# A throwaway tanh behind the key norms' square root in a two-layer hybrid decoder trunk

## The chip, the cores and the metric

The kernel runs on one core of a Trainium2 chip. The metric is the time on the device in microseconds, the median of three runs.

## The reference

Two layers on x (256 tokens by 2048, fp32). Each layer has a token mixer and a squared-ReLU MLP, each between two RMS norms. One input projection feeds both halves of the mixer: RWKV-7 (16 heads of 64) and causal attention (8 heads of 128). What matters here is the part that computes a head's keys and decays:

```python
w_log = -jax.nn.softplus(-(w0 + jnp.tanh(wd) @ w2)) - 0.5
decay = jnp.exp(-jnp.exp(w_log.astype(f32)))
a = jax.nn.sigmoid(a0 + ad @ a2)
g = jax.nn.sigmoid(gd) @ g2
...
kk = heads(k * k_k)
kk = kk / jnp.maximum(jnp.sqrt(jnp.sum(kk * kk, axis=-1, keepdims=True)), 1e-12)
k = k * (1 + (a - 1) * k_a)
rh, kh, vh, ah = heads(r), heads(k), heads(v), heads(a)
y = wkv7_scan(rh, heads(decay), kh, vh, -kk, kk * ah)
...
yn = ((y - mu) * lax.rsqrt(var + LNX_EPS)).reshape(bsz, s, c)
```

The key norm and the norm of y need a square root, the decay and the learning rate a sigmoid (written as a tanh) and exps, the attention an exp.

## The kernel before

Every engine's program is written out by hand, one block each, with semaphores between them; each engine works through its own program in order. Weights come by DMA (SyncE's queue) into a ring of four slots, `raw`, of 128x1024 fp32. Per slot, ScalarE makes `whi`, a rounded copy (`hi`, L892), VectorE makes the rest `wlo = raw - whi` (`lo`, L1156), and TensorE (PE) multiplies with both (`tick`, L514, L515 and L517). A slot's `lo` waits for its `hi`, PE waits for both.

The mixer of a layer goes through 8 pairs of RWKV heads, each together with one attention head: the first 7 pairs in a loop, the last written out. While the chain of small operations of pair i runs (`mixer`, a function of this name for each engine), PE fills its time with the input projection of pair i's last group and of pair i+1: 48 ticks over 12 weight slots, a few at each place (`fill`). The calls `step(-1)` to `step(10)` put the 12 `hi` on ScalarE's queue and the 12 `lo` on VectorE's, between the operations of the chain. `finish` empties two PSUM banks of the projection: ScalarE copies one part into `xl` (`halves`, L900), VectorE adds the other (`sums`, L1162), which lets PE write the banks again (`tile_out`).

At the end of pair i, ScalarE does the softmax's exps (L1030), a throwaway one-column square root (L1033), two copies, the square and the root of y's norm (L1039, L1041), and then `key_norms(n + 1)`, the root of the next pair's key norms (L968). Behind it come `step(8)`, `step(9)`, the attention output (L1046), `step(10)` and, once VectorE has gated y, the copy of L1057. The next pair begins with `step(-1)`, `finish(-1)` and the two tanh (L979, L982), three in layer 1 (L985), then three exps (L987 to L989).

VectorE's order at the same place: the norm of y (to L1425), `step(8)`, the gating (L1438, L1440), the attention's low part (L1429), the low part of y (L1446), `step(9)`, `step(10)`; in the next pair `finish(-1)` (L1162), the clamp (L1265) and the reciprocal (L1267) of the key norms, then L1270, the first user of the tanh, the scan (L1272), and the chain that ends at L1309 with what PE transposes at L649. In each layer `key_norms` is called once before the loop as well, for the first pair. PE's order: the ticks of the last group, the small lora matmuls (L628 to L630, in layer 1 L632 too), then seven ticks that wait for `tile_out`, then L639 and L649.

The key-norm root and the tanh of the next pair use different tables of ScalarE; the instruction that loads one (ACT_TABLE_LOAD) is put in by the compiler, in front of the activation that needs it, and bears its line. `spare` is a 128x1 tile that nothing reads; `col_eps` is a constant column.

Of the kernel before, what the change touches and what calls it, by code (L numbers as in the profile page):

```python
# [32 lines left out]
ACT = mybir.ActivationFunctionType  # L33
# [74 lines left out]
def trunk(nc, consts, levels, x, norm_mix_pre, norm_mix_post, norm_mlp_pre, norm_mlp_post, w_in, w_in_vres,  # L108
          shift_mu, shift_mu_vres, decay_w0, decay_w2, iclr_a0, iclr_a2, vres_v0, vres_v2,
          gate_g2, k_k, k_a, r_k, lnx_gain, lnx_bias, w_out, w_up, w_down, out):  # L110
    with ExitStack() as ctx:
        def sb(name, shape, dt=F32):
            return ctx.enter_context(nc.sbuf_tensor("b_" + name, shape, dt))
# [51 lines left out]
        spare = sb("spare", [P, 1])  # L165
# [21 lines left out]
        col_eps, col_lnx = cst[:, C_COL + 2:C_COL + 3], cst[:, C_COL + 3:C_COL + 4]  # L187
# [693 lines left out]
        def _(act):  # L881
            f = nc.scalar.activation
# [82 lines left out]
            def key_norms(n):  # L965

                act.wait_ge(e["n2_sum"], n + 1)
                f(rn[:, :], mb[0][:, SEQ:2 * SEQ], ACT.Sqrt).then_inc(e["n2_root"], 1)  # L968

            def mixer(l, i, n, tiles, step, finish, more=True):  # L970

# [70 lines left out]
                if more:  # L1042
                    key_norms(n + 1)
# [19 lines left out]
            for l in range(DEPTH):  # L1063
# [17 lines left out]
                def turn(i):  # L1081
                    def finish(g):

                        halves(k + 11 + 4 * g, i * 3, t + 4 + 2 * g + i * 6, (2, 2, 0)[g + 1])
                    mixer(l, i, PAIRS * l + i, t + 4 + i * 6, lambda j: hi(k + 8 + j + LEAD, i * 3), finish)
                key_norms(PAIRS * l)
                loop(act, PAIRS - 1, turn)

# [543 lines left out]
```

## Time and profile before

| | |
|---|---|
| median of three runs | 2646.45 us |
| lowest, highest | 2644.17, 2647.09 us |
| the profiled execution's own time | 2645.33 us |
| its span, first to last instruction | 2643.7 us |
| its mean granted clock of TensorE | 0.994 |
| busy share: PE, VectorE, ScalarE, GpSimd | 98%, 64%, 46%, 4% |
| weights and other data moved by DMA | 419.96 MB, mean 159 GB/s |

All rows below are of one profiled execution. PE's busy time overlaps itself, since matmuls are pipelined and their ends are modelled; so the waits of PE are read rather than its busy time. A timeline's row gives the start and the duration, both in microseconds; instructions of one line that follow each other are merged ("x2"). On ScalarE and VectorE an instruction may start a little before the one ahead of it ends.

### The profile page before, as it was taken

What the parts mean: (1) busy time and instruction counts of PE and PEld (TensorE: products, weight loads), DVE (VectorE), ACT (ScalarE), POOL (GpSimd) and SP (SyncE); (2) the same over time, 40 slices, a digit from 0 to 9 for tenths busy, and PEclk for the clock granted to TensorE, in tenths of its full rate; (3) what the DMA queues carried; (4) which work ended last, traced back from release to release, by engine and by line L of the source; (5) the groups of instructions that cost most, each with busy time, mean ns of one, the idle gap of its engine ahead of it and who ended that gap; (6) DMA issues with size and microseconds to landing.
All of it is one profiled execution on the core that took longest, in us unless ns stands there. A gap on an engine that the chain in (4) does not pass through costs nothing.

```text
span 2643.7 us, 48415 instructions
## 1 busy us (share of the span) xinstructions
PE 2585.5 (98%) x16267; PEld 2118.7 (80%) x16267; DVE 1680.0 (64%) x2761; ACT 1210.2 (46%) x1896; POOL 116.4 (4%) x183
## 2 busy tenths in 40 slices
PE   7999999999999999999899999999999999999998
PEld 6777777778888888888687777777788888888886
DVE  5767666657656556566567766676576565564665
ACT  5444445445434444344454444454454344443443
POOL 3000000000000000000010000100000000000000
PEclk9999999999999999999999999999999999999999
DMA  6443333365555555555544333333655655555554
GB/s 199 117 117 110 108 105 97 122 216 174 189 192 184 192 188 183 200 183 191 171 117 119 106 113 105 97 98 120 215 175 190 192 183 192 190 181 199 185 189 150
DMA packets 437898, 419.96 MB, mean 159 GB/s; under 512 B 19503, under 2 KB 351937, under 8 KB 437825
## 3 DMA queue, kind: packets, MB, share of 16 engines
q1 hardware_dynamic: 434176, 412.49, 49.1%
q0 software_dynamic: 3648, 6.52, 0.9%
q8 instruction: 44, 0.72, 0.1%
q14 instruction: 30, 0.24, 0.0%
HBM read 416.84 MB, written 2.10 MB: 158 GB/s over the span
## 4 chain that ended last, share of the span: by engine, by line
PE 91%; DVE 6%; ACT 1%; issue 1%; DMA 0%; DVEq 0%; SPq 0%; ACTq 0%
PE gemm_bank L514 29%; PE gemm_bank L515 15%; PE gemm_bank L539 11%; PE gemm_bank L541 11%; PE gemm_bank L540 11%; PE gemm_bank L517 2%; PE mix_banks L661 1%; PE mix_banks L687 1%; DVE b_rn L1267 1%; DVE b_wlo L1156 1%; PE mix_banks L694 1%; PE mix_banks L733 1%; PE mix_banks L737 1%; PE mix_banks L744 1%; PE mix_banks L740 1%
## 5 line engine op out<-in xcount | busy, mean ns | idle before, releaser
L1156 DVE TENSOR_TENSOR b_wlo<-b_raw,b_whi 128x1024 fp32r<-128x1024 f32 x777 | 940.2, 1223 | 561.0 <-ACT b_whi L892 558.8
L514 PE MATMUL gemm_bank<-b_hT,b_whi 128*128 128x512 f32 x3420 | 1253.5, 407 | 2.2 <-DVE b_zt L1162 2.2
L892 ACT ACTIVATE b_whi<-b_raw 128x1024 fp32r<-128x1024 f32 x777 | 810.1, 1057 | 609.2 <-PE gemm_bank L541 428.4
L515 PE MATMUL gemm_bank<-b_hT,b_wlo 128*128 128x256 f32 x3648 | 1012.7, 281 | 0.0
L514 PEld LDWEIGHTS gemm_bank<-b_hT,b_whi 128*128 128x128 f32 x3420 | 643.2, 188 | 171.3 <-issue 22.4
L515 PEld LDWEIGHTS gemm_bank<-b_hT,b_wlo 128*128 128x128 f32 x3648 | 689.5, 189 | 10.7
L539 PE MATMUL gemm_bank<-b_whi,b_mT 128*128 128x512 f32 x1280 | 501.6, 392 | 0.0
L541 PE MATMUL gemm_bank<-b_whi,b_mT 128*128 128x512 f32 x1280 | 498.3, 389 | 0.0
L540 PE MATMUL gemm_bank<-b_wlo,b_mT 128*128 128x512 f32 x1280 | 498.2, 389 | 0.0
L539 PEld LDWEIGHTS gemm_bank<-b_whi,b_mT 128*128 128x128 f32 x1280 | 240.3, 188 | 51.3 <-issue 1.4
L541 PEld LDWEIGHTS gemm_bank<-b_whi,b_mT 128*128 128x128 f32 x1280 | 240.3, 188 | 50.3
L540 PEld LDWEIGHTS gemm_bank<-b_wlo,b_mT 128*128 128x128 f32 x1280 | 240.3, 188 | 48.7
L900 ACT ACTIVATE b_xl<-gemm_bank 128x256 f32<-128x256 f32 x229 | 75.1, 381 | 149.1 <-PE gemm_bank L517 145.1
L1021 ACT ACTIVATE b_U<-mix_banks 64x128 f32<-64x128 f32 x64 | 17.4, 271 | 223.9 <-PE mix_banks L733 223.9
L1115 ACT ACTIVATE b_mT<-b_AR 128x256 f32 (+1 forms) x128 | 48.3, 418 | 111.8 <-DVE b_AR L1561 111.8
L1002 ACT ACTIVATE b_yo<-mix_banks 128x256 f32<-128x256 f32 x80 | 30.7, 384 | 143.1 <-PE mix_banks L694 143.1
L1555 DVE TENSOR_TENSOR b_AR<-gemm_bank,b_xl 128x256 f32<-128x256 f32 x128 | 48.5, 420 | 62.2 <-ACT b_xl L900 62.1
L517 PE MATMUL gemm_bank<-b_hT,b_whi 128*128 128x512 f32 x228 | 85.1, 395 | 0.0
L1565 DVE TENSOR_TENSOR b_mT<-b_AR,b_mT 128x256 f32 (+1 forms) x128 | 50.9, 424 | 26.4 <-ACT b_mT L1115 25.9
L1162 DVE TENSOR_TENSOR b_zt<-gemm_bank,b_xl 128x256 f32<-128x256 f32 x101 | 38.2, 420 | 37.8 <-ACT b_xl L900 37.0
L687 PEld LDWEIGHTS mix_banks<-b_yo 64*64 64x64 f32 x1280 | 44.6, 134 | 21.1 <-issue 21.1
L694 PE MATMUL mix_banks<-b_yo 64*64 64x64 f32 x1536 | 60.8, 225 | 0.0
(238 smaller groups left out, 1895.8 us busy)
## 6 DMA issues: line engine op xcount, KB each, us to landing
b_raw<-in_w_up SPq DMA_DIRECT2D x256, 512.0 KB
b_raw<-in_w_down SPq DMA_DIRECT2D x256, 512.0 KB
b_raw<-in_w_in SPq DMA_DIRECT2D x384, 256.0 KB
b_raw<-in_w_out SPq DMA_DIRECT2D x60, 512.0 KB
b_raw<-in_w_in SPq DMA_DIRECT2D x8, 512.0 KB
b_xt<-in_x SPq DMA_DIRECT2D x4, 512.0 KB, 6.0
b_raw<-in_w_out SPq DMA_DIRECT2D x8, 256.0 KB
out<-b_xt SPq DMA_DIRECT2D x8, 256.0 KB, 2.3
```

What stands on the lines that cost most here:

```text
L514: mm(bank[b0 + b][:, :], whi[r][:, cols], pair, start=first, stop=False)
L515: m = mm(bank[b0 + b][:, 0:SEQ], wlo[r][:, cols], act[:, kt, 0, :], start=False, stop=False)
L517: m = mm(bank[b0 + b][:, :], whi[r][:, cols], pair, start=False, stop=True)
L539: mm(bank[b0 + u][:, :], mT[:, kt, 0, toks], whi[r][:, cols], start=first, stop=False)
L540: mm(bank[b0 + u][:, :], mT[:, kt, 0, toks], wlo[r][:, cols], start=False, stop=False)
L541: m = mm(bank[b0 + u][:, :], mT[:, kt, 1, toks], whi[r][:, cols], start=False, stop=last)
L687: mm(mb[2 + h][to, CHUNK * u:CHUNK * u + CHUNK], old, Z[rows, lv, 2 * h + u, :], start=True, stop=True)
L694: m = mm(mb[h][to, CHUNK * u:CHUNK * u + CHUNK], Z[rows, lv, 2 * h + u, :], old, start=True, stop=True)
L892: f(whi[r][:, :], raw[r][:, :, :].rearrange("p a b -> p (a b)"), ACT.Copy).then_inc(hi_done, 1)
L900: f(xl[:, b, :], bank[b0 + b][:, SEQ:2 * SEQ], ACT.Copy).then_inc(half_out, 1)
L1156: tt(wlo[r][:, :], flat(raw[r][:, :, :]), whi[r][:, :].bitcast(F32), ALU.subtract).then_inc(lo_done, 1)
L1565: tt(mT[:, at, 1, :], hid(b).unsqueeze(1), mT[:, at, 0, :].bitcast(F32), ALU.subtract).then_inc(tile_out, 1)
```

## The change

One line is added to `key_norms` on ScalarE: a tanh of one constant column into `spare`, behind the root. It signals nobody. It runs wherever `key_norms` is called: once before the loop of each layer, and in each of the 7 loop turns, so 16 times.

```diff
                 act.wait_ge(e["n2_sum"], n + 1)
                 f(rn[:, :], mb[0][:, SEQ:2 * SEQ], ACT.Sqrt).then_inc(e["n2_root"], 1)
+                f(spare[:, :], col_eps, ACT.Tanh)
 
             def mixer(l, i, n, tiles, step, finish, more=True):
```

## Rows read from the trace of the kernel before

**Rows 1.** The page: busy time of each engine; chain that ended last, by engine.
```profile
PE 2585.5 (98%) x16267; PEld 2118.7 (80%) x16267; DVE 1680.0 (64%) x2761; ACT 1210.2 (46%) x1896; POOL 116.4 (4%) x183
...
PE 91%; DVE 6%; ACT 1%; issue 1%; DMA 0%; DVEq 0%; SPq 0%; ACTq 0%
```

**Rows 2.** Groups of instructions by line (columns as in the page), ScalarE.
```profile
L979 ACT ACT_TABLE_LOAD x16 | 20.5, 1283 | 0.3
```

**Rows 3.** Timeline, ScalarE, one seam: start, duration (us), instruction, [idle before <- releaser].
```profile
282.00 0.19 ACT L1030 ACTIVATION_READ_ACCUMULATOR b_sm<-b_sm,b_small 128x1 f32 x1
282.21 1.28 ACT L1033 ACT_TABLE_LOAD   x1
...
283.71 0.38 ACT L1035 ACTIVATE b_AKV<-mix_banks 128x256 f32<-128x256 f32 x1
...
285.48 0.36 ACT L968 ACTIVATE b_rn<-mix_banks 128x256 f32<-128x256 f32 x1
285.74 2.00 ACT L892 ACTIVATE b_whi<-b_raw 128x1024 fp32r<-128x1024 f32 x2
...
287.90 1.06 ACT L892 ACTIVATE b_whi<-b_raw 128x1024 fp32r<-128x1024 f32 x1
288.97 0.42 ACT L1057 ACTIVATE b_mT<-b_yf 128x256 f32 x1
...
291.98 0.66 ACT L900 ACTIVATE b_xl<-gemm_bank 128x256 f32<-128x256 f32 x2 [1.53 <-PE gemm_bank L517]
292.66 1.28 ACT L979 ACT_TABLE_LOAD   x1
293.95 0.47 ACT L979 ACTIVATE b_eN<-mix_banks,b_drv 128x256 f32<-128x256 f32 x1
```

**Rows 4.** Timeline, VectorE, the same seam.
```profile
286.82 1.23 DVE L1156 TENSOR_TENSOR b_wlo<-b_raw,b_whi 128x1024 fp32r<-128x1024 f32 x1 [0.58 <-ACT b_whi L892]
...
289.64 0.42 DVE L1446 TENSOR_TENSOR b_mT<-b_yf,b_mT 128x256 f32 x1 [0.47 <-ACT b_mT L1057]
289.98 2.35 DVE L1156 TENSOR_TENSOR b_wlo<-b_raw,b_whi 128x1024 fp32r<-128x1024 f32 x2
292.40 0.76 DVE L1162 TENSOR_TENSOR b_zt<-gemm_bank,b_xl 128x256 f32<-128x256 f32 x2
...
293.39 1.75 DVE L1267 RECIPROCAL b_rn<-b_rn 128x256 f32<-128x256 f32 x1
295.06 0.23 DVE L1270 TENSOR_SCALAR b_ldc<-b_eN 128x256 f32<-128x256 f32 x1
```

**Rows 5.** Timeline, TensorE matmuls, the same seam.
```profile
288.87 0.40 PE L514 MATMUL gemm_bank<-b_hT,b_whi 128*128 128x512 f32 x1
...
293.41 0.47 PE L514 MATMUL gemm_bank<-b_hT,b_whi 128*128 128x512 f32 x1 [0.29 <-DVE b_zt L1162]
```

**Rows 6.** Timelines, VectorE and TensorE, start of layer 0's first pair.
```profile
59.59 0.76 DVE L1162 TENSOR_TENSOR b_zt<-gemm_bank,b_xl 128x256 f32<-128x256 f32 x2 [4.05 <-ACT b_xl L900]
...
60.60 0.47 PE L514 MATMUL gemm_bank<-b_hT,b_whi 128*128 128x512 f32 x1 [0.48 <-DVE b_zt L1162]
```

**Rows 7.** Timeline, VectorE, a seam of layer 1.
```profile
1428.96 2.35 DVE L1156 TENSOR_TENSOR b_wlo<-b_raw,b_whi 128x1024 fp32r<-128x1024 f32 x2
1431.44 0.76 DVE L1162 TENSOR_TENSOR b_zt<-gemm_bank,b_xl 128x256 f32<-128x256 f32 x2
```

**Rows 8.** Waits of TensorE: who was waited for, total us, times, longest.
```profile
PE mix_banks L649 <- DVE b_btl L1309: 7.1, 8, 1.0
```

**Rows 9.** TensorE's timeline; stretches (length, busy us by engine, clock, DMA share, GB/s).
```profile
593.33 1.09 PE L563 MATMUL mix_banks<-b_cst,b_xt 128*128 128x128 f32 x8 [3.10 <-DVE b_xt L1176]
...
595.00:595.50 0.50, 0.50 (x5) 0.50 (x4) 0.50 (x2) 0.50 (x2) 0.00 (x0) 0.50 0.00 0
601.50:602.00 0.50, 0.50 (x5) 0.46 (x4) 0.50 (x3) 0.50 (x1) 0.50 (x1) 0.87 0.17 33
234.00:292.00 58.00, 57.53 (x499) 44.70 (x497) 40.69 (x89) 26.74 (x53) 3.85 (x7) 1.00 0.38 111
```

## The prediction

> **What bounds the kernel now.** I read the page first: TensorE (PE) is busy for 98% of the span, VectorE (DVE) for 64%, ScalarE (ACT) for 46%, and the chain that ended last is PE for 91% and DVE for 6% [rows 1]. So time spent or saved on ScalarE is worth something only at a place where PE waits, at the end of some chain, for ScalarE. Next, the groups of instructions on ScalarE: a table load takes 1283 ns each time, and 16 of them stand before the tanh at L979, one for each pair of heads, 8 pairs in each of 2 layers [rows 2]. In the seam a second one stands before the throwaway square root at L1033, and the copies behind either have none [rows 3], so copies run on either table. Then the timelines of the three engines around one seam between two pairs, the one at 283 to 296 us, which is where the change acts [rows 3 to 5]. The reader should look there for instructions that start within some hundredths of a microsecond of the end of what they wait for: those have no slack, and whatever delays the one delays the other.
>
> The chain at the seam. ScalarE does the key norms' square root (L968) and then at once the conversion `hi` of weight slot 8 (L892, at 285.74, ends near 286.80) [rows 3]. VectorE has been idle for 0.58 us for it and starts the matching `lo` (L1156) at 286.82 [rows 4]. VectorE's queue is in order: behind that `lo` stand the gating of the pair's output, the split of L1446, two more `lo`, then the two sums that empty the PSUM banks (L1162, 292.40), the clamp and the reciprocal of the key norms (L1267), and only then the line that needs the tanh (L1270) [rows 4]. PE, at 293.41, has been idle for 0.29 us for L1162 [rows 5], because its next group of weights overwrites those banks. So hi(8), lo(8), the tail of VectorE, L1162 and PE form one chain.
>
> **The change part by part.** *What is added:* behind each of the 16 key-norm roots, a table load and a one-column tanh. The nearest row is the same pair of instructions with a square root, at L1033: the load starts at 282.21, 0.02 us after its predecessor ends (282.00 + 0.19), and the instruction behind the throwaway one starts at 283.71, so 1.52 us go by from the end of the one to the start of the next [rows 3]. Without the pair, the next instruction begins 0.10 us before its predecessor ends (L968 ends at 285.48 + 0.36 = 285.84, L892 starts at 285.74) [rows 3]. So hi(8) comes 1.52 + 0.10 = 1.62 us later; the lower bound is 1.50, load and tanh alone, with none of the overlap lost.
>
> *What is removed:* the load of L979, since its table is now in place when the next pair begins. There are as many loads as before: 16 are moved, none is dropped. What it is worth must be read where the tanh is used. In the seam the tanh ends at 293.95 + 0.47 = 294.42, but L1270 starts at 295.06, just when the reciprocal releases VectorE (293.39 + 1.75 = 295.14, with the usual 0.08 of overlap) [rows 3, 4]. The tanh is 0.64 us early already; coming 1.28 us earlier still, it is worth nothing. The a-tanh and the exps come behind, and wait for VectorE too.
>
> *Is 1.62 us absorbed on the way?* ScalarE has 1.53 us idle before its L900 [rows 3], and that hides its own lateness there almost wholly, but it is the wrong place: the loss is passed on to VectorE 6 us before that, through lo(8). On VectorE the 0.58 us before lo(8) is the wait itself. The idle time before L1446 (0.47) is a wait for ScalarE's L1057, which stands behind hi(10) (287.90 + 1.06 = 288.96, start 288.97) [rows 3, 4]; hi(10) is 1.62 later as well. Two `lo` then run to 289.98 + 2.35 = 292.33, could give way at 292.25 with the overlap of 0.08, and L1162 starts at 292.40 because the first half of L900 ends near 292.36 [rows 3, 4]: slack 0.15. In layer 1 the same working gives 1428.96 + 2.35 − 0.08 = 1431.23 against 1431.44, slack 0.21 [rows 7]. I take these two for all loop seams of their layers.
>
> *What else is late.* PE needs lo(8) for the last 16 matmuls of its group, which start near 288.9 [rows 5]. lo(8) now ends at 286.82 + 1.23 = 288.05, and would end at 289.67, so PE stops there for 0.8 us, and L900 moves from 291.98 to about 292.8. Its first half is ready near 293.2, before VectorE is free at 292.25 + 1.62 = 293.87, so this stall doesn't add; it is part of the same 1.62. The load of the next weights into the slot is issued after lo(8), so 1.6 us later, and is used after L1270, which is as late. The normalised output that PE transposes (L785) needs no ScalarE work behind the new tanh. So nothing else grows.
>
> *Layer 0, 7 loop seams:* PE waits for L1162 already [rows 5], thus 1.62 − 0.15 = 1.47 us each. *Layer 1, 7 loop seams:* PE has a fourth small matmul and doesn't wait at L1162, but it waits some 0.9 us (7.1 / 8) for VectorE at L649, 8 times in this trace, the longest 1.0 us [rows 8], so there VectorE's lateness arrives whole: 1.62 − 0.21 = 1.41 us each. *The first pair of each layer, 2 times:* hi and L900 follow L968 on ScalarE, VectorE sits idle for 4.05 us until L900 and PE 0.48 us until VectorE [rows 6]: no slack, 1.62 us each. The sum: 7 × 1.47 + 7 × 1.41 + 2 × 1.62 = 10.3 + 9.9 + 3.2 = 23.4 us.
>
> Nothing is given back later: between seams PE is busy for 57.53 of 58 us [rows 9], so there is no idle time that a late start could use up. The profiled execution took 2645.33 us (span 2643.7), 1.1 less than the median of 2646.45; the sum on the profiled one is 2668.7, on the median 2669.9. I predict 2669.9.
>
> *A rule against the row.* The rows show a load of 1.28 us with neighbours 0.01 to 0.02 us away on both sides [rows 3]. The Trainium skill, ScalarE: Activation LUTs, section What ACT_TABLE_LOAD costs, puts a drain of some 1380 ns beside each load, 2.66 us for a switch; an estimate from that page would make each seam 1.38 us worse and the whole change some 22 us worse again, near 2692 us in all. The trace doesn't show such a drain, so I don't add it.
>
> **The rivals.**
> *Faster, with the tanh as the last to arrive:* the change would gain if, at L1270, VectorE waited for the tanh, and if the load at its new place fell in idle time. Then the 1.28 us of each load goes: 16 × 1.28 = 20.5 us, 2626 us. For it: ScalarE's 1.53 us idle before L900. Against it: the 0.64 us by which the tanh is early, and lo(8) 0.02 us behind hi(8). It decides where hi(8) is needed 1.6 us later than it is done. Chance 0.03.
>
> *Hidden:* the delay of lo(8) is swallowed by VectorE before L1162, which it can do only if the 0.47 and 0.58 us of idle are no consequence of ScalarE. No gain, no loss: 2646 us. Chance 0.07. Partly hidden (one idle time of the two, about 0.5 us in each loop seam): 14 × 0.5 = 7 us less, 2663; chance 0.05.
>
> *The table load stays at L979 too* (the change doesn't do what it says, because the table isn't known at the loop's head): then ScalarE has 1.28 us more, but the tanh would end near 293.4 + 1.28 + 0.47 = 295.1, against 296.6 when the late VectorE wants it. The time is the forecast's, the loads are up to 16 more. If instead the throwaway tanh were dropped, the time would be 2646; the one at L1033 is kept, so this is in "hidden".
>
> *Costlier, by the clock:* PE's granted clock fell from 1.00 to 0.50 (2.4 to 1.2 GHz) after a stop of 3.10 us that ended at 593.33: it was 0.50 at 595.0 and nearly back in the slice from 601.5 [rows 9]. At most 6.5 us of matmuls ran at half of the clock, which costs up to 3.3 us; I take 2.5, since part of it was idle. If a stop of about 1.9 us, in two pieces, did this at every seam, it would add 16 × 2.5 = 40 us: 2710. Against it: each piece is at most a good third of that stop (0.8 and 1.1 against 3.10), and a whole pair, with its stops at both ends, runs at a granted clock of 1.00 now [rows 9]. Chance 0.05.
>
> **How the numbers follow.** Forecast 0.80, partly hidden 0.05, costlier 0.05, hidden 0.07, faster 0.03. The forecast's own bounds: with 1.50 inserted instead of 1.62 the sum is 1.9 less; with no slack at all 2.5 more; and the runs of the kernel before lie up to 2.3 from their median: 2666 to 2675. With the partly hidden case the range is 2661 to 2676. Faster by over 0.2% (what a measurement of this kernel can tell from no change) 0.03, within it 0.07, slower 0.90.
>
> **What would show it.** Right: 16 loads at the new line, none at L979; VectorE's idle time before lo(8) at each loop seam 0.58 + 1.62 = 2.2 us instead of 0.58; PE idle before its first L514 some 1 us instead of 0.29 and a new stop of 0.8 us near the end of the group before it; L1270 straight behind the reciprocal; each pair 1.4 to 1.5 us longer. Wrong: if VectorE's L1162 starts less than 1 us later against the pair's own root, something on VectorE had slack that I took for a wait on ScalarE; if L1270 comes to wait for the tanh, the tanh's place in the chain was misread; if the clock's row shows less than 1.00 between pairs, the last rival.

## The result, and the profile after

The changed kernel takes 2668.47 us (median of four runs, 2666.64 to 2669.13), against 2646.44 for the kernel before: 22.0 us more, a ratio of 1.0084 with a 95% interval of 1.0066 to 1.0101. It is slower, by about what was forecast (2669.9). The profiled execution took 2666.64 us, its span is 2665.0, so between the two profiled executions there are 21.3 us. The times of the experiments below are medians too; the kernel before, run anew beside them, took 2646.43 us beside e1 to e4 and 2646.88 beside e5 to e8, and their ratios are to these.

The first look is ScalarE's timeline at the seam that answers to [rows 3] (a row is start, duration, instruction, idle time before). Lines from L969 on have moved down by one, so L979 of before is L980 here, and VectorE's L1156, L1162, L1267 and L1270 are L1157, L1163, L1268 and L1271.

```profile
292.81 0.36 ACT L968 ACTIVATE b_rn<-mix_banks 128x256 f32<-128x256 f32 x1
293.19 1.28 ACT L969 ACT_TABLE_LOAD   x1
294.49 0.20 ACT L969 ACTIVATE b_spare<-b_cst 128x1 f32<-128x1 f32 x1
294.60 1.99 ACT L892 ACTIVATE b_whi<-b_raw 128x1024 fp32r<-128x1024 f32 x2
...
300.19 0.66 ACT L900 ACTIVATE b_xl<-gemm_bank 128x256 f32<-128x256 f32 x2 [0.88 <-PE gemm_bank L517]
300.82 0.47 ACT L980 ACTIVATE b_eN<-mix_banks,b_drv 128x256 f32<-128x256 f32 x1
```

The load now stands behind the root, and none stands between L900 and L980. hi(8) starts 1.79 us after the root starts (294.60 − 292.81); it was 0.26 [rows 3]. The same places on VectorE, which answer to [rows 4]:

```profile
295.67 1.23 DVE L1157 TENSOR_TENSOR b_wlo<-b_raw,b_whi 128x1024 fp32r<-128x1024 f32 x1 [2.09 <-ACT b_whi L892]
...
298.49 0.43 DVE L1447 TENSOR_TENSOR b_mT<-b_yf,b_mT 128x256 f32 x1 [0.46 <-ACT b_mT L1058]
298.83 2.35 DVE L1157 TENSOR_TENSOR b_wlo<-b_raw,b_whi 128x1024 fp32r<-128x1024 f32 x2
301.10 0.75 DVE L1163 TENSOR_TENSOR b_zt<-gemm_bank,b_xl 128x256 f32<-128x256 f32 x2
...
302.09 1.75 DVE L1268 RECIPROCAL b_rn<-b_rn 128x256 f32<-128x256 f32 x1
303.76 0.23 DVE L1271 TENSOR_SCALAR b_ldc<-b_eN 128x256 f32<-128x256 f32 x1
```

The wait before lo(8) has grown from 0.58 to 2.09 us. L1163 now follows the two `lo` with the usual small overlap (298.83 + 2.35 − 0.08 = 301.10), so the slack before it is used up. L1271 still stands straight behind the reciprocal, while the tanh ended at 301.29: it is 2.47 us early instead of 0.64, and nobody uses that. TensorE's timeline there, which answers to [rows 5], and its waits over the whole execution (who was waited for, total us, times, longest), where the L649 row is that of [rows 8] unchanged:

```profile
297.05 0.47 PE L514 MATMUL gemm_bank<-b_hT,b_whi 128*128 128x512 f32 x1 [0.68 <-DVE b_wlo L1157]
...
302.11 0.47 PE L514 MATMUL gemm_bank<-b_hT,b_whi 128*128 128x512 f32 x1 [0.78 <-DVE b_zt L1163]
```
```profile
PE gemm_bank L514 <- DVE b_wlo L1157: 9.5, 14, 0.7
PE gemm_bank L514 <- DVE b_zt L1163: 8.5, 9, 2.0
PE mix_banks L649 <- DVE b_btl L1310: 7.1, 8, 1.0
PE mix_banks L639 <- DVE b_t L1283: 2.7, 13, 0.3
```

The first row is new: 14 loop seams, 0.68 us each. The second was 2.2 us before, and the last 0.9 us (5 times). The groups of instructions on ScalarE show the moved loads, as many as in [rows 2]:

```profile
L969 ACT ACT_TABLE_LOAD x16 | 20.5, 1283 | 0.3
```

The best measure of a cost per pair is the time from one root (L968) to the next, since all loop turns of a layer are alike. It is worked out from the starts of that line; the 7 intervals of a layer are the first pair and 6 loop turns.

| us per pair | first pair, layer 0 | loop turns, layer 0 | first pair, layer 1 | loop turns, layer 1 |
|---|---|---|---|---|
| before | 52.97 | 58.20 | 54.11 | 59.35 |
| after | 55.58 | 59.59 | 55.60 | 60.66 |
| difference | 2.61 | 1.39 | 1.49 | 1.31 |

These 14 intervals make 20.3 of the 21.3 us. The seventh seam of each layer lies outside them: that of layer 0 in the stretch to the first root of layer 1 (910.3 us in both kernels), that of layer 1 behind the last root (863.5 us to the end, against 863.1). The last 0.5 us stand before the first root, where the change has done nothing yet.

### The profile page after: what moved, and what is told of

Read it like the earlier page. It is cut to its first block, busy times and chain, and to the rows that moved or that the text cites. A ratio compares the mean times of both kernels' runs of the same rounds, so it can differ in the third digit from the quotient of the medians.

```text
span 2665.0 us, 48431 instructions
## 1 busy us (share of the span) xinstructions
PE 2588.7 (97%) x16267; PEld 2119.1 (80%) x16267; DVE 1678.0 (63%) x2761; ACT 1213.4 (46%) x1912; POOL 116.6 (4%) x183
## 4 chain that ended last, share of the span: by engine, by line
PE 86%; DVE 6%; ACT 5%; issue 2%; DVEq 0%; DMA 0%; SPq 0%; ACTq 0%
PE gemm_bank L514 27%; PE gemm_bank L515 14%; PE gemm_bank L539 11%; PE gemm_bank L541 11%; PE gemm_bank L540 11%; PE gemm_bank L517 2%; ACT b_whi L892 2%; DVE b_wlo L1157 1%; PE mix_banks L661 1%; PE mix_banks L687 1%; DVE b_rn L1268 1%; PE mix_banks L694 1%; PE mix_banks L733 1%; ACT L1034 1%; PE mix_banks L744 1%
## 5 line engine op out<-in xcount | busy, mean ns | idle before, releaser
L1157 DVE TENSOR_TENSOR b_wlo<-b_raw,b_whi 128x1024 fp32r<-128x1024 f32 x777 | 939.9, 1223 | 583.5 <-ACT b_whi L892 581.5
L514 PE MATMUL gemm_bank<-b_hT,b_whi 128*128 128x512 f32 x3420 | 1254.9, 407 | 18.4 <-DVE b_wlo L1157 9.5
L514 PEld LDWEIGHTS gemm_bank<-b_hT,b_whi 128*128 128x128 f32 x3420 | 643.0, 188 | 191.0 <-issue 28.5
L900 ACT ACTIVATE b_xl<-gemm_bank 128x256 f32<-128x256 f32 x229 | 75.1, 380 | 140.9 <-PE gemm_bank L517 136.9
L1556 DVE TENSOR_TENSOR b_AR<-gemm_bank,b_xl 128x256 f32<-128x256 f32 x128 | 48.4, 419 | 62.2 <-ACT b_xl L900 62.1
L1163 DVE TENSOR_TENSOR b_zt<-gemm_bank,b_xl 128x256 f32<-128x256 f32 x101 | 38.1, 419 | 40.2 <-ACT b_xl L900 40.2
```

What stands on the lines that cost most here:

```text
L514: mm(bank[b0 + b][:, :], whi[r][:, cols], pair, start=first, stop=False)
L900: f(xl[:, b, :], bank[b0 + b][:, SEQ:2 * SEQ], ACT.Copy).then_inc(half_out, 1)
L1157: tt(wlo[r][:, :], flat(raw[r][:, :, :]), whi[r][:, :].bitcast(F32), ALU.subtract).then_inc(lo_done, 1)
```

## The experiments

My theory is the prediction's: the whole cost is the delay of hi(8), and the load taken away in front of the tanh was worth nothing, because the tanh wasn't last. The rivals: the freed load was worth its 1.28 us (and the other place cost that much more), or a load costs more than its row wherever it stands. The Trainium skill, ScalarE: Activation LUTs, section What ACT_TABLE_LOAD costs, states such a cost, a drain of 1380 ns.

**The same tanh where ScalarE is idle (e1).**

```diff
                 step(-1)
+                f(spare[:, :], col_eps, ACT.Tanh)
                 finish(-1)
```

This is the kernel before with that line in ScalarE's mixer, and nothing behind the root.

> The kernel before with the same throwaway tanh at another place: not behind the key norms' root but in the next pair, between the first hi (step(-1)) and the copies of L900, where ScalarE has 1.46 to 1.56 us idle in each loop seam. The load in front of the tanh of L979 goes, as in the change. Theory (the delay of hi(8) is the whole cost, the removed load is worth nothing): 1.50 us fit the idle time in 14 seams, the two first pairs have no idle time and cost 1.5 us each: 2646.4 + 3 = 2649.5 us. Rival 1 (an earlier tanh is worth its 1.28 us): 2649.5 less up to 18, some 2632 us. Rival 2 (a table load costs wherever it stands outside the tanh's line, for a drain or the like): near 2668 us.

It took 2650.72 us, a ratio of 1.0017 (1.0007 to 1.0026). ScalarE's timeline at the seam, where L980 is again the tanh:

```profile
292.70 1.06 ACT L892 ACTIVATE b_whi<-b_raw 128x1024 fp32r<-128x1024 f32 x1
293.78 1.28 ACT L976 ACT_TABLE_LOAD   x1
295.08 0.20 ACT L976 ACTIVATE b_spare<-b_cst 128x1 f32<-128x1 f32 x1
295.29 0.66 ACT L900 ACTIVATE b_xl<-gemm_bank 128x256 f32<-128x256 f32 x2
295.93 0.47 ACT L980 ACTIVATE b_eN<-mix_banks,b_drv 128x256 f32<-128x256 f32 x1
```

The load has filled the 1.53 us that ScalarE had idle in front of L900. The loop turns take 58.23 and 59.39 us, against 58.20 and 59.35: nothing is lost and, with every tanh 1.3 us earlier (7.15 us behind its root instead of 8.47), nothing is won. So the freed load is worth nothing, and a load put into idle time costs nothing. What is left sits in the two first pairs, 2.7 and 2.5 us longer, where there is no idle time; that is 1 us more each than the 1.5 I expected, and in both of them the clock fell (below).

**One more load (e2).**

```diff
                 f(spare[:, 0:1], col_eps, ACT.Tanh)
+                f(spare[:, 1:2], col_eps, ACT.Sqrt)
```

> The changed kernel with a throwaway square root behind the throwaway tanh. So one more load stands in front of hi(8) and the load in front of the next pair's tanh is back. Theory: 1.50 us more at the place on the chain, with no slack left there, 16 times, and nothing for the load that is back: 2668.5 + 24 = 2692.5 us. Rival (the removed load was worth its 1.28 us, and the change's cost was the larger for it): 2692.5 + 16 x 1.28 = 2713 us. Rival 2 (a drain of 1.38 us beside each load): 2713 to 2735 us.

It took 2700.62 us, 32 more than the changed kernel; I had expected 24, the rivals 44 or more. ScalarE behind the root:

```profile
303.25 0.20 ACT L969 ACTIVATE b_spare<-b_cst 128x1 f32<-128x1 f32 x1
303.46 1.28 ACT L970 ACT_TABLE_LOAD   x1
304.75 0.20 ACT L970 ACTIVATE b_spare<-b_cst 128x1 f32<-128x1 f32 x1
304.86 1.99 ACT L892 ACTIVATE b_whi<-b_raw 128x1024 fp32r<-128x1024 f32 x2
```

The second pair of instructions adds 1.50 us, as its row says, and there is no drain between the tanh and the load behind it: 0.01 us. The loop turns split into two kinds. Of layer 0's six, three take 61.05 to 61.09 us, 1.5 more than after; the other three take 62.15 to 62.18, 1.1 more again. The stretches of the execution (length, busy us by engine, granted clock, DMA share, GB/s) show the second kind's reason, here behind a stop of PE of 2.18 us for lo(8), which ended at 121.89:

```profile
121.00:122.00 1.00, 0.11 (x1) 0.14 (x2) 1.00 (x2) 1.00 (x3) 0.00 (x0) 1.00 0.00 0
122.00:123.00 1.00, 1.00 (x5) 0.92 (x6) 0.84 (x3) 0.98 (x2) 0.00 (x0) 0.80 0.00 0
123.00:124.00 1.00, 1.00 (x5) 0.81 (x5) 0.66 (x2) 0.99 (x2) 0.00 (x0) 0.50 0.58 154
```

PE's clock fell to 0.50 just after PE was busy again, and stayed there for some 3.4 us. The mean granted clock of the execution is 0.987, against 0.995 after. In layer 1 four of the six loop turns are the slow kind (63.0 to 63.3 us against 62.2). The profiled execution is 35.7 us longer than that of the changed kernel, so 11.7 are to be explained beyond the 24. Seven turns of 0.8 to 1.1 us make 7.1. Between the layers are 2.2 (914.0 us from the last root of layer 0 to the first of layer 1, against 910.3, of which 1.5 is the load) and behind the last root 1.8; the clock fell at the seam there too. Another 0.8 stands before the first root. So the theory's price holds for the seams at full clock, and the rival by the clock, which I had at 5% for the change itself, is real with the longer stop of 2.18 us.

**A copy instead of the tanh (e3).**

```diff
                 f(rn[:, :], mb[0][:, SEQ:2 * SEQ], ACT.Sqrt).then_inc(e["n2_root"], 1)
+                f(spare[:, :], col_eps, ACT.Copy)
```

> The kernel before with a throwaway one-column copy behind the key norms' root in place of the tanh: the same instruction at the same place, but no table load with it. Theory: 0.1 to 0.2 us at each place, of which the slack of 0.15 to 0.21 before L1162 takes most: 2646.4 to 2648 us. Rival (it is the instruction behind the root, not the load, that costs, for instance by ending the overlap of root and hi): over 2655 us.

2646.01 us, a ratio of 0.9999 (0.9990 to 1.0009). The instruction alone delays hi(8) by 0.09 us and costs nothing that can be measured; so it is the load in it that costs.

**How early was the tanh (e4, e5)?** Both get 15 one-column copies in front of the tanh, e4 in the kernel before and e5 in the changed one:

```diff
+                for j in range(1, 16):
+                    f(spare[:, j:j + 1], col_eps, ACT.Copy)
                 act.wait_ge(e["lora_w"], V)
                 f(eN[:, :, :].rearrange("p a b -> p (a b)"), mb[0][:, 0:SEQ], ACT.Tanh, bias=half(HALF),
```

> The kernel before with 15 throwaway one-column copies between L900 and the tanh of L979: a delay of the tanh alone of about 1.5 to 1.7 us (0.1 us each behind one another, by the overlap seen). Theory: the tanh was 0.64 us early, so it is now last by 0.9 to 1.1 us in all 16 pairs: 2646.4 + 14 to 18 = 2661 to 2664 us. Rival (the tanh has no slack): + 24 to 27, 2672 us. Rival 2 (PE or VectorE hides it wholly): 2646.4 us.

> The changed kernel with the same 15 throwaway copies between L900 and the next pair's tanh. In the changed kernel's trace the tanh ends at 301.29 and its user starts at 303.76, so it is 2.47 us early. Theory: 1.5 to 1.7 us are hidden wholly: 2668.5 us, within 2. Rival (the tanh's early arrival is what limits the loss): over 2680 us.

e4 took 2659.61 us, 13.2 more than before; e5 took 2667.82, the changed kernel's time. In e4 VectorE's user of the tanh has begun to wait for it (L1272 is L1270 of before):

```profile
298.05 1.75 DVE L1269 RECIPROCAL b_rn<-b_rn 128x256 f32<-128x256 f32 x1
300.50 0.29 DVE L1272 TENSOR_SCALAR b_ldc<-b_eN 128x256 f32<-128x256 f32 x1 [0.69 <-ACT b_eN L981]
```

The copies took 1.50 us and with the overlap delayed the tanh by 1.4. Its user starts 0.77 us later behind the root (10.35 against 9.58 us), so some 0.6 were hidden, and a loop turn became 0.87 and 0.91 us longer. That is at or just under the lower end of my 0.9 to 1.1, and the sum of 13.2 just under my 14 to 18; both are far from the rivals' 0 and 1.5 us a pair. In e5 the same copies delay the tanh by 1.3 us and are hidden wholly. So there was slack of some 0.6 us in front of the tanh's user before, and in the changed kernel there is more than 1.3 (2.47 by the rows): the change gained time where nobody waited for it, and paid where there was no slack.

**The reciprocal in VectorE's longer gap (e6).** The changed kernel, with clamp and reciprocal as a helper, `key_inverse`, which runs once before the loop of each layer as well:

```diff
-                dve.wait_ge(e["n2_root"], V)
-                ts(rn[:, :], rn[:, :], 1e-12, None, ALU.max).then_inc(e["n2_max"], 1)
-                dve.wait_ge(e["n2_max"], V)
-                nc.vector.reciprocal(rn[:, :], rn[:, :]).then_inc(e["n2_inv"], 1)
...
+                if more:
+                    key_inverse(n + 1)
                 step(8)
```

> The changed kernel, with VectorE's clamp and reciprocal of the next pair's key norms (0.28 + 1.75 us) moved from behind L1163 into VectorE's idle time before lo(8), which the change made 2.09 us long. Theory: lo(8), L1163 and the start of PE's next group stay where they are, but the tanh's user comes 2.0 us earlier, so PE's waits at L649 (7.1 us in all) and L639 (2.7 us) go: 2668.5 - 9 = 2659 to 2661 us. Rival 1 (the reciprocal doesn't stand in the chain): 2668.5 us. Rival 2 (lo(8) moves later by it): over 2670 us.

2654.29 us, 14.2 less than the changed kernel and still slower than before (1.0028, 1.0017 to 1.0038); I had expected 2659 to 2661, too little of a gain. The two fit the gap, and L1273, the tanh's user, now follows the sums at once:

```profile
291.80 1.75 DVE L1262 RECIPROCAL b_rn<-b_rn 128x256 f32<-128x256 f32 x1
293.65 1.23 DVE L1157 TENSOR_TENSOR b_wlo<-b_raw,b_whi 128x1024 fp32r<-128x1024 f32 x1
...
299.08 0.75 DVE L1163 TENSOR_TENSOR b_zt<-gemm_bank,b_xl 128x256 f32<-128x256 f32 x2
299.75 0.28 DVE L1273 TENSOR_SCALAR b_ldc<-b_eN 128x256 f32<-128x256 f32 x1
```

So the reciprocal was what held L1271. PE's waits at L649 and L639 (9.8 us together) are gone, as expected; the gain is 4.4 us larger. Loop turns are 0.49 us shorter in layer 0 and 1.58 in layer 1, where the waits that went make 0.2 and 1.1. The rest is in PE's rows too: its list of waits understates what a wait costs. This is layer 0's seam in the changed kernel, then in e6:

```profile
306.92 0.28 PE L515 MATMUL gemm_bank<-b_hT,b_wlo 128*128 128x256 f32 x1
307.39 0.70 PE L639 MATMUL mix_banks<-b_t,b_cst 128*128 128x256 f32 x2 [0.19 <-DVE b_t L1283]
307.74 0.58 PE L514 MATMUL gemm_bank<-b_hT,b_whi 128*128 128x512 f32 x1
```
```profile
304.90 0.28 PE L515 MATMUL gemm_bank<-b_hT,b_wlo 128*128 128x256 f32 x1
305.02 0.60 PE L639 MATMUL mix_banks<-b_t,b_cst 128*128 128x256 f32 x2
305.27 0.58 PE L514 MATMUL gemm_bank<-b_hT,b_whi 128*128 128x512 f32 x1
```

Without the wait, L639 starts 0.12 us behind the start of the matmul before it and overlaps it; with the wait 0.47 us behind it. The two L639 then take 0.70 us instead of 0.60, and the L514 after them starts 0.45 us later. The wait is entered as 0.19, because the overlap that it ends isn't counted. So the wait at L639 costs 0.45 to 0.5 us in layer 0, and the two in layer 1 cost 0.57 and 1.01; that is the whole difference of the loop turns. (Both first pairs are 1.6 us shorter; in that of layer 0 the clock didn't fall this time. The stretch between the layers is 1.6 us longer, with the clock at 0.50 for 10.2 us there instead of 3.4.)

**VectorE's order changed in the kernel before (e7), and the tanh of e1 on top (e8).** e7 puts the clamp into the 0.58 us before lo(8), lo(9) before L1446, and in layer 1 half of the reciprocal before L1162:

```diff
+                if more:
+                    clamp(n + 1)
                 step(8)
...
                 if more:
                     attention_lo()
+                    step(9)
...
                 step(10)
+                if more and l:
+                    invert(n + 1, 0, P)
```

> The kernel before with VectorE's order at the seam changed and nothing on ScalarE: the clamp goes into the 0.58 us idle before lo(8), lo(9) goes before L1446 (0.47 us idle), and in layer 1 half of the reciprocal goes before L1162. Theory: in layer 1 the chain from L1162 to L1309 is 1.0 us shorter and PE's 0.9 us at L649 go, less some 0.1 at L1162; in layer 0 0.1 us a pair: 2646.4 - 6 to 8 = 2638.5 to 2640.5 us. Rival (L1162 comes late by the half reciprocal and eats it): 2644 to 2650 us.

> e7 with the throwaway tanh of e1 before L900. Theory: in e7 the tanh is the last to arrive in layer 1 by some 0.3 us at most, so the freed load is worth 0 to 2 us in all there, against 3 us for the two first pairs: 2639 to 2643 us, 1 to 3 more than e7. Rival (with VectorE's chain shorter the earlier tanh is worth its 1.28 us in layer 1, 9 us): under 2634 us.

e7 took 2639.71 us, a ratio of 0.9973 (0.9961 to 0.9984) to the kernel before, and is thus faster than both kernels, as expected, though the parts came out otherwise: a loop turn is 0.26 us shorter in layer 0, where I had 0.1, and 0.47 in layer 1, where I had some 0.9. e8 took 2639.67 (0.9974, 0.9963 to 0.9984), not the 1 to 3 us more than e7 that I expected. Their equal times hide two things. In layer 1, e7's row for the tanh's user shows a wait that wasn't there before:

```profile
1431.29 0.94 DVE L1262 RECIPROCAL b_rn<-b_rn 128x128 f32<-128x128 f32 x1
1432.58 0.29 DVE L1275 TENSOR_SCALAR b_ldc<-b_eN 128x256 f32<-128x256 f32 x1 [0.35 <-ACT b_eN L979]
```

and e8's doesn't:

```profile
1437.59 0.94 DVE L1263 RECIPROCAL b_rn<-b_rn 128x128 f32<-128x128 f32 x1
1438.45 0.23 DVE L1276 TENSOR_SCALAR b_ldc<-b_eN 128x256 f32<-128x256 f32 x1
```

With VectorE's chain shorter, the tanh is last, and the freed load is worth 0.51 us a turn in layer 1 (58.37 against 58.88 us), more than the 0 to 0.3 I expected and less than its 1.28. It is about the part that e7 lacked in layer 1. The two first pairs give it back: 55.56 and 56.61 us against 52.69 and 53.62. That is 2.9 and 3.0 us, but the profiled execution (2643.93 us) was e8's slowest, and the clock fell in both of its first pairs; without that they would cost about 1.5 each, an estimate from the changed kernel's 1.49. In layer 0 the turns are alike (57.93 and 57.94). So the idea of the change has a value once the tanh is made the last to arrive, at a place where its load is hidden; here both effects cancel in the medians.

## Why the prediction was right

The mechanism was right, and one term a little too large. **What bounds the kernel** and **the chain at the seam** held: the wait of VectorE before lo(8), PE's new stop near the end of the group (0.68 us, forecast 0.8) and its wait before the next group (0.78, forecast about 1) are all in the rows after, and e3 and e1 show that it is the load, and its place, that costs.

**What is added** was mis-sized by a little. I had 1.62 us, by counting a lost overlap of 0.10 with the 1.52 us; the wait before lo(8) grew by 1.51 (2.09 − 0.58). The row shows why: hi(8) starts at 294.60, 0.09 before the small tanh ends (294.49 + 0.20), so it overlaps that instead of the root. At L1033, from which I took the row, the next instruction didn't overlap. With 1.51 the sum's terms are 1.51 − 0.15 = 1.36 in layer 0 and 1.51 − 0.21 = 1.30 in layer 1; the loop turns measured 1.39 and 1.31. With 1.51 for each first pair the whole sum is 21.6 us instead of 23.4.

**What is removed** was worth nothing, as worked out from the 0.64 us; e4 measures that slack, and e5 shows that there is more of it in the changed kernel.

**Is it absorbed, what else is late:** the slack of 0.15 and 0.21 us was all, and the stop at lo(8) didn't add, as argued. Layer 1's lateness did arrive whole, but one step earlier than I had it: PE is 1.30 us late already at L639, whose entry in the list of waits, for both layers, grew from 0.9 to 2.7 us, and so the wait at L649 is the same 7.1 us.

**The first pairs** I had at 1.62 each; layer 1's cost 1.49, layer 0's 2.61. The 1.1 us beyond the load were not a step of the forecast but the rival by the clock, at one place. TensorE stands still for 1.99 us there, and in the stretches of the changed kernel its clock then falls while it works:

```profile
62.00:63.00 1.00, 0.35 (x2) 0.34 (x3) 0.96 (x4) 0.61 (x2) 0.53 (x1) 1.00 0.00 0
63.00:64.00 1.00, 1.00 (x6) 0.82 (x5) 1.00 (x1) 0.00 (x0) 0.98 (x3) 0.62 0.00 0
64.00:65.00 1.00, 1.00 (x5) 0.90 (x4) 0.97 (x3) 0.00 (x0) 0.72 (x2) 0.50 0.18 45
65.00:66.00 1.00, 1.00 (x5) 0.81 (x4) 1.00 (x2) 0.70 (x2) 0.00 (x0) 0.50 0.25 86
66.00:67.00 1.00, 1.00 (x6) 0.86 (x5) 1.00 (x4) 1.00 (x3) 0.00 (x0) 0.67 0.00 0
```

I had this rival as all or nothing, at 16 seams and 2.5 us each. It came at one, and cost 1.1. The opposite happened at the norm in the middle of layer 0, where the kernel stops in any case: the clock was at 0.50 there from 594.8 to 601.7 in the kernel before [rows 9] and only from 606.0 to 609.4 in the changed one:

```profile
606.00:607.00 1.00, 0.75 (x4) 0.76 (x5) 1.00 (x3) 0.00 (x0) 0.00 (x0) 0.50 0.13 43
609.00:610.00 1.00, 0.72 (x5) 0.48 (x3) 1.00 (x4) 0.99 (x4) 0.00 (x0) 0.81 0.03 8
```

That goes with some 1.4 us given back (the time from the last root of layer 0 to the first of layer 1 is 910.3 us in both, though one seam lies in it). In layer 1 it is the same, 6.8 us at 0.50 before and 3.4 after, and of the seam behind the last root only 0.4 us are seen. So part of the closeness of 22.0 to 23.4 us is luck: the clock took 1.1 us and gave some 2.3 back, and 0.5 us stand before the first root; the loop turns, which no clock disturbed, are the firmer evidence.

**The rule against the row**, the drain beside each load of the Trainium skill, ScalarE: Activation LUTs, What ACT_TABLE_LOAD costs, is not borne out here: the load starts 0.01 to 0.02 us behind its neighbour in e1, e2 and after, and the measured step per load and throwaway instruction is 1.50 us.

## What to carry to other kernels

Moving a table load is worth what the consumer of the activation was waiting for, and costs what stands behind the load at its new place: look first at whether the user of the result starts when its input is ready or when its own engine is free; here the second came 0.64 us after the first. A throwaway activation goes into a stretch where the engine is idle (the 1.53 us before L900 here, where it cost the loop turns nothing, though the two first pairs, which have no such stretch, still made the kernel 4.3 us slower), not merely behind the last use of the old table. And an engine at 46% can be in series with one at 98%: an instruction that starts 0.02 us behind what it waits for says so. In the same way a wait of 0.2 us in PE's list can cost 0.45, since PE's matmuls otherwise overlap: the starts of the rows around it tell.

## What the hardware showed that I had not expected

TensorE's granted clock fell from 1.00 to 0.50 (2.4 to 1.2 GHz) at stops of 1.35 to 3.5 us at the start of a pair, for 3.4 or 6.8 us, and most of the pairs where it did took about 1 us longer. The shortest such stop is in e1's first pair of layer 1, here PE's row and two stretches:

```profile
1377.98 0.77 PE L514 MATMUL gemm_bank<-b_hT,b_whi 128*128 128x512 f32 x1 [1.35 <-DVE b_zt L1163]
```
```profile
1376.00:1377.00 1.00, 0.63 (x3) 0.23 (x2) 0.03 (x1) 0.99 (x4) 0.00 (x0) 0.90 0.00 0
1377.00:1378.00 1.00, 0.02 (x1) 0.05 (x1) 0.97 (x4) 1.00 (x4) 0.19 (x1) 0.50 0.00 0
```

It isn't regular. The stop of 1.35 us in the first pair of layer 1 came with the fall in e1 and e8 and without it in the changed kernel and e6; the stop of 1.99 us in that of layer 0 came with it in the changed kernel and without it in e6; of the 14 stops of 2.18 us in e2, 8 did. What decides it the runs don't show. The 14 loop seams of the changed kernel, with a stop of 0.68 us and in layer 0 another of 0.78, never had it.
